# Two layers on one core: the input arrives in column quarters, the first weight slot in halves, and the values' projection takes its low-part products last

## The chip, the cores and the metric

The kernel runs on one core of one Trainium2 chip. The metric is the device time of one execution in microseconds (us). TensorE is the matrix engine, VectorE (DVE in the rows) and ScalarE (ACT) are the elementwise engines, GpSimd (POOL) and SyncE (SP) issue transfers here, and GpSimd does some elementwise work as well.

## The reference, cut to what matters

The input x is 512 tokens by 1024 columns, float32. Two layers follow each other: a mixer (short convolution and dilated attention) with a gated feed-forward part, and then a second hybrid layer (state-space mixer and sparse attention). The change touches the first steps of the first layer only:

```python
h = rms_norm(x, g_mix)                      # per token, times a gain per column
z = h @ w_in                                # 1024 -> 3072 columns
u, gb, gc, q, k, v = jnp.split(z, splits, axis=-1)
q = rms_norm(q.reshape(B, S, N_HEADS, HEAD_DIM), g_q) * HEAD_DIM ** -0.5
k = rms_norm(k.reshape(B, S, N_HEADS, HEAD_DIM), g_k)
```

## The kernel before

**Layout.** Activations stand transposed: `hH` and `hL` hold 8 blocks (index k, `KD` = 8, `KH` = 4) of 128 columns of h on the partitions and all 512 tokens along the free side. `hH` is the block rounded to the type that TensorE multiplies, `hL` what the rounding left. Weights are split the same way: a slot is 128 output columns of a matrix, 128 x 1024 numbers in `raw[par]`; ScalarE's `split_hi` writes `wH[par]` and counts `hi_done`, VectorE's `split_lo` writes `wL[par]` and counts `lo_done`. A projection of a slot is 8 blocks of three products of 128x512: wH by hH, wH by hL, wL by hH. The queries' columns are slot 0, the keys' slot 1, the values' slot 2; slots 3 and on belong to `mix`. The two buffers of each kind are used in turn.

**The norm.** The root of each token's mean square is not applied to x. It is worked out beside the projections (`squares` on VectorE, lines 1241 to 1247 on ScalarE, `newton`), laid on a diagonal (`diag4`), spread over all partitions by one product on TensorE (line 871, in `row_factors`), copied out by ScalarE as `rb` (and squared as `r2b`), and multiplied into the results (`scaled`).

**The transposes.** x arrives by tokens: `x_tok` has 4 tiles (index t, `TB` = 4) of 128 tokens. `x_turn(t, ks)` waits for the transfer of the tile's half and transposes the 128x128 pieces ks into bank `HB[k]`. Block k is complete when the piece of tile 3 is in; then `xn_mm` is counted, ScalarE writes `hH[:, k]` (line 1234, counted in `h1h`), VectorE writes `hL[:, k]` (line 1717, counted in `h1_done`), and TensorE may take its products. `x_copy(k)` takes a copy of the untouched block into `xT`, on ScalarE (counted in `xt_a`) or, for k = 1, on VectorE (`xt_d`). There are only 7 free banks: `HB[7]` is `HB[0]` again, so piece 7 waits until `x_copy(0)` is through.

**Fillers.** Between the first transposes TensorE transposes the identity into a bank that nobody reads (`transposes(PB[6], [ident] * 2)`), and before them it multiplies a tile of ones (line 746).

**Order.** Every engine runs its own list in the order written, and stops at a wait. SP's list: identity, slot 0 (512 KB), columns 0 to 511 of the four tiles (256 KB each), columns 512 to 1023 of the four tiles, slot 1, then a wait for the last tile, slot 2, eleven small rows. GpSimd issues its first transfers after the same wait. TensorE's list: fillers and x_turn of the first half; pieces 4 to 6 of tiles 0 and 1; `project_first` (slot 0: the lines 850 to 852; pieces 4 to 6 of tiles 2 and 3 ahead of block 2, the four pieces 7 ahead of block 4); `project_second` (slot 1: 16 products with wH, lines 860 and 861, then the 8 with wL, line 864); `row_factors` (lines 871 to 877); slot 2 by `project` (lines 655 to 657, three products a block); a small product (line 885) that waits for seven `x_copy` of ScalarE, and `head_sums(0)` (line 770), which take the squares of queries and keys; then `mix(0)` with slot 3.

**ScalarE's list** there: split_hi of slot 0, the eight hH with x_copy(0) behind the fourth, split_hi of slot 1, two rows of squares, two small steps, split_hi of slot 2, x_copy of 3, 2 and 7, then rb, r2b, the squares of queries and keys, split_hi of slot 3, x_copy of 4, 5 and 6. **VectorE's list**: split_lo of slot 0, the eight hL, x_copy(1), two rows of squares, split_lo of slot 1, the steps of the root, diag4, split_lo of slot 2, scaled queries and keys, some small steps, split_lo of slot 3.

Of the kernel before, what the change touches and what calls it, by code (L numbers as in the profile page):

```python
# [16 lines left out]
F32 = mybir.dt.float32  # L17
# [111 lines left out]
def program(nc, io):  # L129
# [7 lines left out]
    with ExitStack() as ctx:  # L137
# [10 lines left out]
        def sem(name):  # L148
# [121 lines left out]
        cst_in, mask_in, glu_full, vec_in, vecp_in, svec_in, s5_in, out_done = (  # L270
            sem(n) for n in ("cst_in", "mask_in", "glu_full", "vec_in", "vecp_in", "svec_in", "s5_in", "out_done"))
# [44 lines left out]
        fin = [sem(f"fin{t}") for t in range(TB)]  # L316
# [46 lines left out]
        def _(sp_):  # L363
# [61 lines left out]
            def at_(i, last):  # L425
# [3 lines left out]
                for e in range(2):  # L429
                    dst = raw[s.par][:].rearrange("p (k e c) -> p k e c", k=KH, e=2)[:, :, e, :]  # L430
                    src = w_glu_2[0].rearrange("(k p) c -> p k c", p=P)[:, :, bass.ds(i * P + e * HALF, P)]
                    sp_.dma_start(dst, src).then_inc(glu_full if e else w_full[s.par], 16)
# [14 lines left out]
            for t in range(TB):  # L447
                sp_.wait_ge(fin[t], 2)
# [176 lines left out]
        def _(pe):  # L625
# [110 lines left out]
            def x_turn(t, ks):  # L736

                pe.wait_ge(x_in[t][ks[0] // KH], 16)
# [98 lines left out]
            def project_first():  # L837

                pe.wait_ge(lo_done, 1)
                pe.wait_ge(vec_cp, 1)  # L840
                for k in range(KD):
                    if k == 2:
                        x_turn(2, range(KH, KD - 1))
                        x_turn(3, range(KH, KD - 1))
                    if k == KH:
                        pe.wait_ge(xt_a, 1)
                        for t in range(TB):
                            x_turn(t, [KD - 1])
                    pe.wait_ge(h1_done, k + 1)
# [5 lines left out]
            def project_second():  # L855

                pe.wait_ge(hi_done, 2)
                pe.wait_ge(xt_d, 1)
                for k in range(KD):
                    mm(PB[1][:], blk(wH[1], k), hH[:, k, :], start=(k == 0), stop=False)  # L860
                    mm(PB[1][:], blk(wH[1], k), hL[:, k, :], start=False, stop=False)
                pe.wait_ge(lo_done, 2)
                for k in range(KD):
                    ins = mm(PB[1][:], blk(wL[1], k), hH[:, k, :], start=False, stop=(k == KD - 1))
# [328 lines left out]
        def _(act):  # L1193
# [30 lines left out]
            def x_copy(k):  # L1224
                act.wait_ge(h1_done, k + 1)
# [24 lines left out]
            for k in (3, 2, 7):  # L1250
                x_copy(k)
# [292 lines left out]
            act.wait_ge(glu_full, 16)  # L1544
# [5 lines left out]
            def att(i, first, last):  # L1550
# [9 lines left out]
                if not last:  # L1560
                    act.wait_ge(glu_full, i * 16 + 32)
# [69 lines left out]
            def token_scale(j, t):  # L1631

                act.wait_ge(r_fin, j + 1)
                A(out_tok[:, t, HALF:D], out_tok[:, t, HALF:D], ACT.Copy, scale=sm[:, 4 + t:5 + t]).then_inc(fin[t], 1)
# [21 lines left out]
        def _(dve):  # L1656
# [833 lines left out]
            def token_scale(t):  # L2490

                TS(out_tok[:, t, 0:HALF], out_tok[:, t, 0:HALF], sm[:, 4 + t:5 + t], None, MU).then_inc(fin[t], 1)
# [32 lines left out]
```

## Time and profile before

| what | value |
|---|---|
| median of 3 runs | 979.25 us (977.92 to 979.74) |
| the profiled execution, its own time | 977.83 us |
| its span, first to last instruction | 976.2 us |
| TensorE busy in it | 963.0 us |
| first product of slot 0 starts | 11.52 us |
| first product of slot 1 / of slot 2 starts | 18.22 / 24.90 us |
| the load for the small product of line 885 starts | 30.61 us |

The profiled execution is 1.6 us longer than its span, which is what lies outside the instructions. Times in a timeline row are the start and the length; of a run of n equal instructions the length runs from the first start to the last end. The matmuls overlap each other, so the distance between two starts, not the length of one, is what a product costs. A bracket at the end of a row says how long the engine stood idle before it and what released it.

### The profile page before, as it was taken

Reading aid. Unit: us, or ns where it says so; the run is one execution under the profiler, and the core shown is the slowest. Engines: PE = TensorE matmul, PEld = TensorE weight load, DVE = VectorE, ACT = ScalarE, POOL = GpSimd, SP = SyncE. Lnnn points to the kernel's source line nnn. Section 1 sums busy time; section 2 is a strip of 40 time slices with the busy share of each in tenths; the row PEclk is TensorE's granted clock in tenths of the full one; section 3 lists DMA queues with packets and bytes.
Section 4 is the critical chain, followed back from the end, with each engine's and each line's share of the span. In section 5 each row is a group of like instructions: output and inputs, shape, how many; then the busy total and the mean of one; then the engine's idle time right before and its main releaser. Section 6 shows DMA issues by size and latency. Waiting matters only on the chain.

```text
span 976.2 us, 13908 instructions
## 1 busy us (share of the span) xinstructions
PE 963.0 (99%) x4623; PEld 776.4 (80%) x4623; DVE 685.5 (70%) x1227; ACT 412.6 (42%) x683; POOL 187.8 (19%) x321
## 2 busy tenths in 40 slices
PE   8999999999999999999999999999999999999996
PEld 7777777687888888888888886888888887677886
DVE  5886795797766666655336568489889876785756
ACT  5564353644323332323221226955652325663234
POOL 3010111120100000187200001745680220100000
PEclk9999999999999999999999999999999999999999
DMA  7346757332653332334322323333233463653222
GB/s 231 112 94 192 208 167 190 74 96 82 182 173 105 95 98 88 104 105 133 137 102 92 102 77 98 97 87 87 60 92 88 120 160 85 146 153 123 86 87 108
DMA packets 143766, 115.13 MB, mean 118 GB/s; under 512 B 5516, under 2 KB 131724, under 8 KB 143724
## 3 DMA queue, kind: packets, MB, share of 16 engines
q1 hardware_dynamic: 135468, 85.88, 29.7%
q0 software_dynamic: 8240, 28.73, 11.0%
q8 instruction: 21, 0.34, 0.1%
q14 instruction: 21, 0.17, 0.1%
q10 hardware_dynamic: 16, 0.00, 0.0%
HBM read 100.44 MB, written 4.20 MB: 107 GB/s over the span
## 4 chain that ended last, share of the span: by engine, by line
PE 95%; DVE 2%; ACT 1%; DMA 1%; issue 0%; SPq 0%; DVEq 0%; ACTq 0%
PE bank L655 19%; PE bank L656 19%; PE bank L657 19%; PE bank L938 4%; PE bank L937 4%; PE bank L939 4%; PE bank L638 2%; PE bank L640 2%; PE bank L639 2%; PE bank L689 2%; PE bank L709 2%; PE bank L1154 1%; PE bank L1152 1%; PE bank L1153 1%; PE bank L824 1%; PE bank L826 1%
## 5 line engine op out<-in xcount | busy, mean ns | idle before, releaser
L655 PE MATMUL bank<-hH,wH 128*128 128x512 f32 x792 | 310.5, 392 | 0.8 <-DVE gt L1980 0.8
L657 PE MATMUL bank<-hH,wL 128*128 128x512 f32 x792 | 308.3, 389 | 0.0
L656 PE MATMUL bank<-hL,wH 128*128 128x512 f32 x792 | 308.2, 389 | 0.0
L1671 DVE TENSOR_TENSOR wL<-raw,wH 128x1024 fp32r<-128x1024 f32 x155 | 195.5, 1262 | 139.5 <-ACT wH L1197 139.2
L1197 ACT ACTIVATE wH<-raw 128x1024 fp32r<-128x1024 f32 x155 | 164.1, 1058 | 289.7 <-PE bank L657 126.2
L655 PEld LDWEIGHTS bank<-hH,wH 128*128 128x128 f32 x792 | 148.7, 188 | 39.1 <-issue 7.9
L657 PEld LDWEIGHTS bank<-hH,wL 128*128 128x128 f32 x792 | 148.7, 188 | 31.0
L656 PEld LDWEIGHTS bank<-hL,wH 128*128 128x128 f32 x792 | 148.7, 188 | 30.1
L937 PE MATMUL bank<-aH,wH 128*128 (+1 forms) x160 | 62.2, 389 | 0.0
L938 PE MATMUL bank<-aL,wH 128*128 (+1 forms) x160 | 62.2, 389 | 0.0
L939 PE MATMUL bank<-aH,wL 128*128 (+1 forms) x160 | 62.2, 389 | 0.0
L1984 DVE TENSOR_TENSOR ut<-bank,r 128x512 f32<-128x512 f32 x22 | 15.2, 691 | 48.9 <-PE bank L657 48.9
L475 POOL DMA_DIRECT2D pTd<-turned x24 | 13.1, 561 | 136.0 <-DVE turned L1820 53.6
L1286 ACT ACTIVATE L<-L,nmx 128x128 f32<-128x128 f32 (+3 forms) x64 | 35.0, 557 | 0.4 <-DVE nmx L1815 0.4
L937 PEld LDWEIGHTS bank<-aH,wH 128*128 128x128 f32 x160 | 30.0, 188 | 6.3
L939 PEld LDWEIGHTS bank<-aH,wL 128*128 128x128 f32 x160 | 30.0, 188 | 6.3
L938 PEld LDWEIGHTS bank<-aL,wH 128*128 128x128 f32 x160 | 30.0, 188 | 6.1
L481 POOL DMA_DIRECT2D mraw<-in_w_mod_dram x24 | 13.3, 554 | 109.7 <-DVE macc L1846 109.7
L548 POOL COPY yaF<-yg 32x128 f32<-32x128 f32 x64 | 33.4, 521 | 2.9
L1197 ACT ACTIVATE aH<-a 128x512 f32 (+1 forms) x22 | 13.9, 632 | 45.2 <-DVE a L1988 45.2
L1153 PE MATMUL bank<-wH,hL 128*128 128x256 f32 (+1 forms) x96 | 30.6, 318 | 0.0
L1154 PE MATMUL bank<-wL,hH 128*128 128x256 f32 (+1 forms) x96 | 30.6, 318 | 0.0
(494 smaller groups left out, 1568.2 us busy)
## 6 DMA issues: line engine op xcount, KB each, us to landing
raw<-in_w_in_dram SPq DMA_DIRECT2D x61, 512.0 KB, 3.6
mraw<-in_w_mod_dram POOLq DMA_DIRECT2D x24, 512.0 KB, 5.1
raw<-in_w_gate_dram SPq DMA_DIRECT2D x22, 512.0 KB, 3.7
raw<-in_w_up_dram SPq DMA_DIRECT2D x22, 512.0 KB, 3.7
raw<-in_w_down_dram SPq DMA_DIRECT2D x22, 512.0 KB, 3.3
raw<-in_w_out_dram SPq DMA_DIRECT2D x16, 512.0 KB, 3.5
pTd<-turned POOLq DMA_DIRECT2D x24, 320.0 KB, 6.9
x_tok<-in_x_dram SPq DMA_DIRECT2D x8, 256.0 KB, 6.2
```

The source lines that it names most:

```text
L548: ins = g.tensor_copy(dst(a, b), src(a, b))
L655: mm(o, a, hH[:, k, :], start=(k == 0), stop=False)
L656: mm(o, a, hL[:, k, :], start=False, stop=False)
L657: ins = mm(o, b, hH[:, k, :], start=False, stop=(k == KD - 1))
L937: mm(PB[d][:], blk(wH[s], d), rh, start=a, stop=False, skip_group_check=True)
L938: mm(PB[d][:], blk(wH[s], d), rl, start=False, stop=False, skip_group_check=True)
L939: ins = mm(PB[d][:], blk(wL[s], d), rh, start=False, stop=False, skip_group_check=True)
L1153: mm(o, hL[:, f, blkc(t)], w, start=False, stop=False, skip_group_check=True)
L1154: ins = mm(o, hH[:, f, blkc(t)], wl, start=False, stop=(f == last), skip_group_check=True)
L1197: return A(o, i_, ACT.Copy, scale=scale)
L1286: ins = A(l, l, ACT.Exp, bias=nmx[:, c:c + 1], scale=-1.0, accum_out=rs[:, c:c + 1])
L1671: TT(wL[s.par][:], raw[s.par][:], wH[s.par][:].bitcast(F32), SU).then_inc(lo_done, 1)
```

## The change

On SP the input comes as columns 0 to 255 of the four tiles, then the first half of slot 0 (blocks k = 0 to 3), columns 256 to 511 of the tiles, the second half of slot 0, and columns 512 to 1023. ScalarE and VectorE split slot 0 by halves, one behind hH and hL of block 0, one behind those of block 3; the counts of `h1h` and `h1_done` move on by one for it, which `h1h_count` and `h1_count` allow for. TensorE turns pieces 0 and 1 of all tiles and 2 and 3 of tiles 0 and 1 ahead of `project_first`, the others inside it: 2 and 3 of tiles 2 and 3 ahead of block 1, 4 to 7 of tile 0 ahead of block 2, of tile 1 ahead of block 3, of tiles 2 and 3 ahead of block 4. ScalarE's x_copy of 3 and 2 moves ahead of hH of block 4, VectorE's x_copy(1) ahead of hL of block 4. Slots 1 and 2 both take their 16 products with wH first and the 8 with wL last, and `row_factors` stands ahead of block 2 of slot 2 and no more between the slots. The counters `glu_full` and `fin` give way to `w_part` and `x_in_fin`, whose later waits are raised by what the new uses count.

```diff
-            load(Slot(N_MIX), cols(w_in, Z_Q))
-            for h in range(2):
+            def query_half(h, done):
+                c = slice(h * KH, h * KH + KH)
+                sp_.dma_start(raw[0][:].rearrange("p (k c) -> p k c", k=KD)[:, c, :], cols(w_in, Z_Q)[:, c, :]).then_inc(done, 16)
+
+            def x_columns(first, n, done):
                 for t in range(TB):
-                    c = slice(h * HALF, h * HALF + HALF)
-                    sp_.dma_start(x_tok[:, t, c], x[0, t * P:(t + 1) * P, c]).then_inc(x_in[t][h], 16)
+                    c = slice(first, first + n)
+                    sp_.dma_start(x_tok[:, t, c], x[0, t * P:(t + 1) * P, c]).then_inc(done(t), 16)
+            x_columns(0, QD, lambda t: x_in[t][0])
+            query_half(0, w_part)
+            x_columns(QD, QD, lambda t: x_in_fin[t])
+            query_half(1, w_full[0])
+            x_columns(HALF, HALF, lambda t: x_in[t][1])
...
             for t in range(TB):
-                x_turn(t, range(KH))
+                x_turn(t, range(KH // 2))
                 transposes(PB[6], [ident] * 2)
-            transposes(PB[6], [ident] * 2)
-            x_turn(0, range(KH, KD - 1))
-            x_turn(1, range(KH, KD - 1))
+            transposes(PB[6], [ident] * 4)
+            for t in range(2):
+                x_turn(t, range(KH // 2, KH))
+                transposes(PB[6], [ident] * 2)
...
             def project_first():
-                pe.wait_ge(lo_done, 1)
                 pe.wait_ge(vec_cp, 1)
                 for k in range(KD):
-                    if k == 2:
-                        x_turn(2, range(KH, KD - 1))
-                        x_turn(3, range(KH, KD - 1))
+                    if k == 1:
+                        x_turn(2, range(KH // 2, KH))
+                        x_turn(3, range(KH // 2, KH))
+                    if k in (2, 3):
+                        pe.wait_ge(xt_a, 1)
+                        x_turn(k - 2, range(KH, KD))
                     if k == KH:
-                        pe.wait_ge(xt_a, 1)
-                        for t in range(TB):
-                            x_turn(t, [KD - 1])
-                    pe.wait_ge(h1_done, k + 1)
+                        x_turn(2, range(KH, KD))
+                        x_turn(3, range(KH, KD))
+                        pe.wait_ge(lo_done, 1)
+                    pe.wait_ge(h1_done, h1_count(max(k, 1)) if k else 2)
...
-            def project_second():
-
-                pe.wait_ge(hi_done, 2)
-                pe.wait_ge(xt_d, 1)
+            def project_low_last(s, bank, between=None):
+
+                pe.wait_ge(hi_done, s.n + 1)
                 for k in range(KD):
...
+                    if k == KH // 2 and between is not None:
+                        between()
...
             project_first()
-            project_second()
-            row_factors()
+            pe.wait_ge(xt_d, 1)
+            project_low_last(Slot(1), PB[1])
             pe.wait_ge(xt_a, 3)
-            project(Slot(2), bank=PB[2])
+            project_low_last(Slot(2), PB[2], row_factors)
...
+            def query_high(h):
+                c = slice(h * HALF, h * HALF + HALF)
+                act.wait_ge((w_part, w_full[0])[h], 16)
+                copy(wH[0][:, c], raw[0][:, c]).then_inc((h1h, hi_done)[h], 1)
...
-            split_hi(Slot(0))
             act.wait_ge(vec_cp, 1)
             for k in range(KD):
                 act.wait_ge(xn_mm, k + 1)
                 A(hH[:, k, :], HB[k][:], ACT.Identity, scale=vec[:, V_GMIX + k:V_GMIX + k + 1]).then_inc(h1h, 1)
+                if k == 0:
+                    query_high(0)
+                if k == 1:
+                    x_copy(0)
                 if k == KH - 1:
-                    x_copy(0)
+                    query_high(1)
+                    x_copy(3)
+                    x_copy(2)
...
-            for k in (3, 2, 7):
-                x_copy(k)
+            x_copy(7)
...
-            split_lo(Slot(0))
+            def query_low(h):
+                c = slice(h * HALF, h * HALF + HALF)
+                dve.wait_ge((h1h, hi_done)[h], 2 - h)
+                TT(wL[0][:, c], raw[0][:, c], wH[0][:, c].bitcast(F32), SU).then_inc((h1_done, lo_done)[h], 1)
...
             for k in range(KD):
-                dve.wait_ge(h1h, k + 1)
+                dve.wait_ge(h1h, h1h_count(k))
                 STT(hL[:, k, :], HB[k][:], vec[:, V_GMIX + k:V_GMIX + k + 1], hH[:, k, :].bitcast(F32), MU, SU
                     ).then_inc(h1_done, 1)
-            x_copy(1)
+                if k == 0:
+                    query_low(0)
+                if k == KH - 1:
+                    query_low(1)
+                    x_copy(1)
```

## Rows read from the trace of the kernel before

**Rows 1.** The page: busy time, share of the span and instructions of TensorE.
```profile
PE 963.0 (99%) x4623; PEld 776.4 (80%) x4623; DVE 685.5 (70%) x1227; ACT 412.6 (42%) x683; POOL 187.8 (19%) x321
```

**Rows 2.** Stages: busy us (count) of each engine, granted clock, DMA share, GB/s.
```profile
2.00:4.00 2.00, 1.73 (x8) 1.73 (x9) 0.22 (x3) 1.32 (x2) 2.00 (x2) 1.00 0.69 183
4.00:6.00 2.00, 2.00 (x10) 1.75 (x10) 0.14 (x1) 0.09 (x1) 0.10 (x1) 1.00 1.05 294
```

**Rows 3.** Stages: the same columns, first products to the last ones of V.
```profile
11.50:30.60 19.10, 19.10 (x88) 15.00 (x86) 16.59 (x28) 15.31 (x27) 5.33 (x10) 1.00 0.60 179
```

**Rows 4.** Timeline of TensorE, us from the start, until the first transposes.
```profile
5.76 0.69 PE L631 MATMUL bank<-cst 128*128 128x128 f32 x2
6.59 0.66 PE L631 MATMUL bank<-cst,x_tok 128*128 128x128 f32 x4
7.08 0.38 PE L631 MATMUL bank<-cst 128*128 128x128 f32 x2
7.30 0.64 PE L631 MATMUL bank<-cst,x_tok 128*128 128x128 f32 x4
...
9.39 0.65 PE L631 MATMUL bank<-cst,x_tok 128*128 128x128 f32 x4 [0.58 <-DMA x_tok<-in_x_dram]
```

**Rows 5.** Timeline of TensorE, from the first product of slot 0 on.
```profile
11.52 0.47 PE L850 MATMUL bank<-hH,wH 128*128 128x512 f32 x1
...
12.98 0.82 PE L631 MATMUL bank<-cst,x_tok 128*128 128x128 f32 x6
13.55 0.48 PE L850 MATMUL bank<-hH,wH 128*128 128x512 f32 x1
...
18.22 0.39 PE L860 MATMUL bank<-hH,wH 128*128 128x512 f32 x1
...
23.67 1.02 PE L871 MATMUL bank<-diag,ones 128*128 128x512 f32 x2
...
24.90 0.50 PE L655 MATMUL bank<-hH,wH 128*128 128x512 f32 x1
```

**Rows 6.** Timeline of the weight loads: the first one behind V.
```profile
30.61 0.30 PEld L885 LDWEIGHTS bank<-sm,identP 128*128 128x128 f32 x2 [0.41 <-ACT xT L1197]
```

**Rows 7.** Timeline of ScalarE: high parts of the input, first copy of it.
```profile
9.82 2.42 ACT L1234 ACTIVATE hH<-bank,vec 128x512 fp32r<-128x512 f32 x4 [2.85 <-PE bank L631]
12.11 0.61 ACT L1197 ACTIVATE xT<-bank 128x512 f32<-128x512 f32 x1
13.62 1.84 ACT L1234 ACTIVATE hH<-bank,vec 128x512 fp32r<-128x512 f32 x3 [0.89 <-PE bank L631]
```

**Rows 8.** Timeline of ScalarE, the row factor out of its bank.
```profile
24.73 0.60 ACT L1197 ACTIVATE rb<-bank 128x512 f32<-128x512 f32 x1 [1.42 <-PE bank L871]
```

**Rows 9.** Timeline of VectorE: low parts of the input, then of weights.
```profile
10.62 2.73 DVE L1717 SCALAR_TENSOR_TENSOR hL<-bank,vec,hH 128x512 fp32r<-128x512 f32 x4 [2.40 <-ACT hH L1234]
14.34 2.79 DVE L1717 SCALAR_TENSOR_TENSOR hL<-bank,vec,hH 128x512 fp32r<-128x512 f32 x4 [0.99 <-ACT hH L1234]
...
20.19 1.22 DVE L1671 TENSOR_TENSOR wL<-raw,wH 128x1024 fp32r<-128x1024 f32 x1
...
25.36 0.69 DVE L1709 TENSOR_TENSOR qraw<-bank,rb 128x512 f32<-128x512 f32 x1 [0.99 <-ACT rb L1197]
...
30.71 1.22 DVE L1671 TENSOR_TENSOR wL<-raw,wH 128x1024 fp32r<-128x1024 f32 x1
```

**Rows 10.** Timeline of the SP queue: first weight slot and the input.
```profile
1.43 0.42 SPq L373 DMA_DIRECT2D raw<-in_w_in_dram  x1
1.90 4.33 SPq L379 DMA_DIRECT2D x_tok<-in_x_dram  x8
```

**Rows 11.** DMA issues, KB each, us from issue to landing: the first weight slot.
```profile
raw<-in_w_in_dram SPq DMA_DIRECT2D x1, 512.0 KB, 4.5
```

**Rows 12.** DMA issues, KB each, us from issue to landing: the first input tile.
```profile
x_tok<-in_x_dram SPq DMA_DIRECT2D x1, 256.0 KB, 4.6
```

**Rows 13.** DMA issues, KB each, us from issue to landing: the last two input tiles.
```profile
x_tok<-in_x_dram SPq DMA_DIRECT2D x2, 256.0 KB, 6.7
```

More of the change, by code:

```diff
@@ L269, in program @@
         x_in = [[sem(f"x_in{t}{h}") for h in range(2)] for t in range(TB)]
-        cst_in, mask_in, glu_full, vec_in, vecp_in, svec_in, s5_in, out_done = (
-            sem(n) for n in ("cst_in", "mask_in", "glu_full", "vec_in", "vecp_in", "svec_in", "s5_in", "out_done"))
+        x_in_fin = [sem(f"x_in_fin{t}") for t in range(TB)]
+        cst_in, mask_in, w_part, vec_in, vecp_in, svec_in, s5_in, out_done = (
+            sem(n) for n in ("cst_in", "mask_in", "w_part", "vec_in", "vecp_in", "svec_in", "s5_in", "out_done"))
         w_full = [sem(f"w_full{s}") for s in range(2)]
@@ L315, in program, with x_part, h1h_count, h1_count @@
             sem(n) for n in ("g_out", "rows_in", "tk_ev", "tk_mm", "x3t", "tsq", "tsum", "f_ln", "f_rs"))
-        fin = [sem(f"fin{t}") for t in range(TB)]
+        def x_part(t, k):
+            return x_in[t][1] if k >= KH else x_in_fin[t] if k >= KH // 2 else x_in[t][0]
+        def h1h_count(k):
+            return 1 if k == 0 else k + 2
+        def h1_count(k):
+            return 1 if k == 0 else k + 2
         def wait(eng, s, v):
@@ L431, in at_ @@
                     src = w_glu_2[0].rearrange("(k p) c -> p k c", p=P)[:, :, bass.ds(i * P + e * HALF, P)]
-                    sp_.dma_start(dst, src).then_inc(glu_full if e else w_full[s.par], 16)
+                    sp_.dma_start(dst, src).then_inc(w_part if e else w_full[s.par], 16)
                 if not last:
@@ L447, in _ @@
             for t in range(TB):
-                sp_.wait_ge(fin[t], 2)
+                sp_.wait_ge(x_in_fin[t], 18)
                 sp_.dma_start(out[0, t * P:(t + 1) * P, :], out_tok[:, t, :]).then_inc(out_done, 16)
@@ L736, in x_turn @@
             def x_turn(t, ks):
-                pe.wait_ge(x_in[t][ks[0] // KH], 16)
+                pe.wait_ge(x_part(t, ks[0]), 16)
                 for k in ks:
@@ L853, in project_first @@
                 ins.then_inc(slot_used, 1)
-            def project_second():
-                pe.wait_ge(hi_done, 2)
-                pe.wait_ge(xt_d, 1)
+            def project_low_last(s, bank, between=None):
+                pe.wait_ge(hi_done, s.n + 1)
                 for k in range(KD):
-                    mm(PB[1][:], blk(wH[1], k), hH[:, k, :], start=(k == 0), stop=False)
-                    mm(PB[1][:], blk(wH[1], k), hL[:, k, :], start=False, stop=False)
-                pe.wait_ge(lo_done, 2)
+                    if k == KH // 2 and between is not None:
+                        between()
+                    mm(bank[:], blk(wH[s.par], k), hH[:, k, :], start=(k == 0), stop=False, skip_group_check=True)
+                    mm(bank[:], blk(wH[s.par], k), hL[:, k, :], start=False, stop=False, skip_group_check=True)
+                pe.wait_ge(lo_done, s.n + 1)
                 for k in range(KD):
-                    ins = mm(PB[1][:], blk(wL[1], k), hH[:, k, :], start=False, stop=(k == KD - 1))
+                    ins = mm(bank[:], blk(wL[s.par], k), hH[:, k, :], start=False, stop=(k == KD - 1), skip_group_check=True)
                 ins.then_inc(slot_used, 1)
@@ L1543, in _ @@
             gate(s, tga[:, KD - 1, :])
-            act.wait_ge(glu_full, 16)
+            act.wait_ge(w_part, 32)
             split_hi(s.next())
@@ L1560, in att @@
                 if not last:
-                    act.wait_ge(glu_full, i * 16 + 32)
+                    act.wait_ge(w_part, i * 16 + 48)
                 split_hi(s.next())
@@ L2490, in token_scale @@
             def token_scale(t):
-                TS(out_tok[:, t, 0:HALF], out_tok[:, t, 0:HALF], sm[:, 4 + t:5 + t], None, MU).then_inc(fin[t], 1)
+                TS(out_tok[:, t, 0:HALF], out_tok[:, t, 0:HALF], sm[:, 4 + t:5 + t], None, MU).then_inc(x_in_fin[t], 1)
             token_last(0)
```

4 lines of the change are left out of this document (2 added, 2 removed).

## The prediction, made before the changed kernel was run

> **What bounds the kernel now.** I read the page first: TensorE is busy 99% of the span [rows 1], so only a change in TensorE's own list, or in the time at which it gets going, can move the end. The stages then show that from the first product of slot 0 to the end of slot 2 TensorE is busy 19.10 of 19.10 us at a granted clock of 1.00 [rows 3]. What lies ahead of 11.52 us is start-up: fillers and transposes [rows 4], and the transfers, which run at 183 and then 294 GB/s [rows 2]. The change wants to shorten this start-up. So I follow TensorE's list, in starts of instructions, from 5.76 to the load at 30.61 us [rows 4 to 6], with the two engines that feed it beside it [rows 7 to 9]. Everything behind 30.61 is taken to shift as a whole.
>
> **Prices from the rows.** Two fillers cost 0.22 us (7.08 to 7.30), four transposes 0.49 (6.59 to 7.08) [rows 4], six transposes queued inside the projection 0.57 (12.98 to 13.55), so 0.095 each; 24 products 5.45 (18.22 to 23.67), so 0.227 each and 0.68 a block; two blocks with an interruption ahead 1.46 (11.52 to 12.98), so 0.78 for the first of them [rows 5]. ScalarE makes hH every 0.60 us (four in 2.42) and takes about 0.60 for a copy of 128x512 [rows 7]; VectorE makes hL every 0.68 (four in 2.73) and takes 0.69 for a 128x512 subtraction or product [rows 9]; half a slot is that size. Behind a queued transpose the chain to TensorE is: six transposes start at 12.98, the piece of block 4 in tile 3 is the fourth, at 13.27; hH at 13.62, hL at 14.34 [rows 5, 7, 9], and hL is usable 0.90 after its start (10.62 to 11.52) [rows 5, 9]: 1.97 us in all. At the start of the kernel it was 9.39 to 11.52, 2.13 [rows 4, 5].
>
> **Do the transfers come in time?** The identity and slot 0, 0.59 MB, had landed at 1.43 + 4.5 = 5.9 us [rows 10, 11]; with the first tile, 0.85 MB, it was 1.90 + 4.6 = 6.5 [rows 10, 12]. In the new order 0.59 MB is the identity and the first quarter of all four tiles, 0.85 MB takes in the first half of slot 0. The quarters take four issues for that instead of one. At 0.5 us an issue (eight in 4.33 [rows 10]) the fourth goes out at about 2.9, and 2.9 plus the 4.5 of rows 11 is 7.4 as an upper bound. TensorE needs tile 0's quarter at 5.98 (5.76 plus two fillers) and tile 3's, behind three lots of two transposes and two fillers (0.25 + 0.22 each), at 7.39. So it is in time, or just. ScalarE needs the first half of slot 0 at 8.4. The last tiles landed at 5.6 + 6.7 = 12.3 [rows 10, 13]; with five more issues (2.3 us) and the same bytes ahead they may come at 12.5 to 14.6, and TensorE asks for them at 15.0 (below). The transfers of the changed order thus bound nothing; slot 1 lands near 14 to 16 and is split at 18.4. Slot 2's transfer now waits for the second half's split (14.2, before 12.3) and has until 22.3; the eleven small rows behind it on SP leave 2 us later and are read near 27. GpSimd's small transfers wait for the same last tile. These I cost at nothing.
>
> By the Trainium skill ("DMA: Bandwidth & Descriptors", Measured under Bandwidth) small transfers are poor ones: batch to 1 MiB, 64 KB reaches 32% of the peak. That speaks against quarters of 128 KB. This trace shows eight transfers of 256 KB in flight together at 294 GB/s and more; the rule is about one at a time, and I weigh it as a rival below.
>
> **First product.** Tile 3's piece at 7.39; hH 0.43 later (9.39 to 9.82), 7.82; hL 0.80 behind (9.82 to 10.62), 8.62, done 9.30 [rows 4, 7, 9]. ScalarE's high half runs 8.42 to 9.02 under that. Then VectorE makes the low half of the slot, 0.65, to 9.95, and TensorE starts 0.22 later (hL started 10.62, plus 0.68, against 11.52): **10.17 us, 1.35 sooner**. TensorE's second lots (tiles 0 and 1) and their fillers end near 9.1 and are hidden.
>
> **Inside project_first.** Here the list of TensorE decides. Before, 10 of the 32 pieces were turned after the first product, each at least two blocks ahead of its use. Now 20 are, some right ahead of the block that the chain behind them releases.
> - Block 0: 10.17 to 10.95. Pieces 2 and 3 of tiles 2 and 3: 0.38; tile 3's piece 2 is the third, at 11.14. Block 1: 11.33 to 12.11. Tile 0, four pieces: to 12.49. Block 2 can't start before 11.14 + 1.97 = 13.11: **a hole of 0.62**.
> - Block 2 to 13.89, tile 1 to 14.27, block 3 to 15.05 (its hL is ready at 13.8). Then eight pieces to 15.81, of which tile 3's piece 4 is the fifth, at 15.43. Block 4 can't start before 17.40: **a hole of 1.59**. I take 17.37 with the roundings.
> - ScalarE has high half, x_copy(3) and x_copy(2) (to 14.8), VectorE low half and x_copy(1) (to 14.9) before that and neither is late. hL of blocks 5 to 7 come every 0.68, TensorE's own pace, so slot 0 ends at 17.37 + 0.78 + 3 x 0.68 = **20.19, before 18.22: 1.97 later**.
> The sum agrees: -1.35, +0.95 for ten more pieces inside, +2.21 for the holes, +0.1 to 0.2 for more interruptions.
>
> **Slots 1 and 2.** Slot 1's 24 products run 20.19 to 25.64. ScalarE's high part is there at 19.4. VectorE, 1.55 later than before (hL 7 at 18.5, then the squares without x_copy(1)), has the low part at 20.19 + 1.22 + 1.55 = 22.96 [rows 9]; it is wanted at 23.8. The low part of slot 2 would come at 25.9, so low-last saves a wait of 0.3 that the old order would have had.
> But row_factors moves behind four products of slot 2 (0.91). It takes 1.23 (23.67 to 24.90) either way. From its product to the load behind slot 2 ScalarE's chain lasted 23.67 to 30.61 = 6.94 us: rb at 24.73, its square, then queries and keys as VectorE delivers them (25.36), the split of slot 3, three copies. Row 6 names the last copy as what released that load, so there is no slack [rows 5, 6, 8, 9]. Now: 25.64 + 0.91 + 6.94 = **33.49**. TensorE is done with slot 2 at 26.55 + 1.23 + 20 x 0.227 + 0.1 = 32.42 and stands **1.07 us**. x_copy of 3, 2 and 7 don't help: they lay ahead of rb. VectorE's list to slot 3's low part (30.71 before) hangs on rb too and shifts alike [rows 9].
>
> **Sum.** 33.49 - 30.61 = +2.88 us. The profiled execution took 977.83 for a span of 976.2; the new one should take 980.7. The median is 979.25, 1.4 above the profiled execution; with the same shift it becomes **982.1 us**. What a measurement can tell from no change is about 0.2%, 1.96 us, so slower is above 981.2.
>
> **Rivals.**
> 1. *The late row factors are hidden*, by a ScalarE list with slack that the profile doesn't show. Then +1.8, 981.05: just no change. Against it: the named releaser and 6.94 us without a pause over 0.3. Chance 0.10.
> 2. *No holes*: the chain from transpose to product is shorter when it is not the first, so that only counts of instructions decide. Then -1.35 + 0.95 + 0.15 + 1.07 = +0.8, 980.1. Against it: the 1.97 has two rows on it at 0.35 and 0.72. Chance 0.12.
> 3. *Faster*: the early start is kept whole, because TensorE's transposes fill waits that it has anyway and ScalarE's chain hides the rest. With -1.35 kept it is 977.9, within 0.2%. It is faster by more only if block 0 starts before 11.52 - 1.96 = 9.56; that would need tile 3's first quarter turned at 6.8, but the list puts three lots ahead of it from 5.98. As a mechanism: the fillers cost less than 0.22 a pair when data is there. Chance 0.08, of a time near 977.
> 4. *The quarters come late*: at half the rate of rows 2, the 0.59 MB need 2.65 us longer, tile 3's quarter lands at 8.6 instead of 5.9, 1.2 behind its need, and all follows: 983.3. Chance 0.06. The skill's rule above gives this case; the rows don't bear it out.
> 5. *The clock falls in the holes*: from 2.4 to 1.2 GHz while TensorE waits 1.59 us, and the 12 products of blocks 4 to 7 take 0.227 longer each: +2.7, 984.8. For it: less work than before up to 17 us. Against it: 1.00 in every row, with 5.9 us of transposes and gaps ahead of 11.52. Chance 0.04. The Trainium skill ("TensorE: Matmul & The Clock Gate", Part 4) says that transposes don't count as busy as matmuls do; by that the clock could have fallen before 11.52 already, and rows 2 and 3 don't show it.
> The forecast has 0.60.
>
> **How the numbers follow.** Own range of the forecast: the holes by a chain of 1.85 to 2.13 (-0.2, +0.3), the first product from 10.0 to 10.9, the wait of 1.07 by 0.3: +2.2 to +4.0, 981.4 to 983.3. The median itself moves by 1 us. The range takes in rivals 1, 2 and 4 and leaves out 3 and 5, with 0.7 us for the measurement at the low end and 1.1 at the high one: 979.4 to 984.4. Slower: 0.56 of the forecast's 0.60, with 0.06 and 0.04 of rivals 4 and 5: 0.66. Same: 0.04, 0.10, 0.12, and a little of rival 3: 0.28. Faster: 0.06.
>
> **What would show it.** First product of slot 0 at 10.0 to 10.4; TensorE idle 0.6 us ahead of block 2 and 1.6 ahead of block 4, released by VectorE's hL; first product of slot 1 at 20.2; load of line 885 at 33.5, idle 1.1 ahead of it, released by an xT copy; the rest of the trace shifted by 2.9. It would be wrong if the first product came under 9.6 or the holes were absent, or if a later stage had slack that took the shift up; no row shows a wait of TensorE for something that doesn't shift along.

## The result, and the profile after

The changed kernel takes 981.49 us in the median of 10 runs (980.56 to 982.77); the kernel before, measured beside it, 979.50 us (977.92 to 982.10, 10 runs). The ratio is 1.0021, with a 95% interval of 1.0013 to 1.0030: 2.0 us slower, 1.3 to 2.9. The forecast was 982.1 in a range of 979.4 to 984.4, slower; 981.49 lies only 0.3 above the 981.2 at which the prediction drew the line between the same and slower. The profiled executions lie further apart than the medians: 981.53 against 977.83 us, spans of 980.0 against 976.2. What the traces say of the extra 1.7 us is told in experiments 5 to 7.

TensorE's timeline after, against [rows 4, 5]. The lines that carry the products of slot 0 are now 873 to 875, those of slots 1 and 2 884 to 888, the factors' product 895, the transposes 651.

```profile
7.55 0.38 PE L651 MATMUL bank<-cst,x_tok 128*128 128x128 f32 x2
...
10.23 0.47 PE L873 MATMUL bank<-hH,wH 128*128 128x512 f32 x1 [0.77 <-DVE wL L1749]
...
11.36 0.48 PE L873 MATMUL bank<-hH,wH 128*128 128x512 f32 x1
...
12.44 0.63 PE L651 MATMUL bank<-cst,x_tok 128*128 128x128 f32 x4
13.06 0.50 PE L873 MATMUL bank<-hH,wH 128*128 128x512 f32 x1
...
14.99 1.03 PE L651 MATMUL bank<-cst,x_tok 128*128 128x128 f32 x8
17.36 0.47 PE L873 MATMUL bank<-hH,wH 128*128 128x512 f32 x1 [1.33 <-DVE hL L1754]
...
20.19 0.39 PE L884 MATMUL bank<-hH,wH 128*128 128x512 f32 x1
...
25.63 0.39 PE L884 MATMUL bank<-hH,wH 128*128 128x512 f32 x1
...
26.55 1.02 PE L895 MATMUL bank<-diag,ones 128*128 128x512 f32 x2
```

Tile 3's first quarter is turned at 7.55 and the first product starts at 10.23, where it was 11.52. Then come the two holes. Block 1 starts at 11.36, its third product at 11.91; at 0.23 us a product TensorE could go on at 12.14. Tile 0's pieces follow at 12.44 only, and block 2 at 13.06. The eight pieces of tiles 2 and 3 start at 14.99, take 0.8, and block 4 starts at 17.36 with 1.33 us of idle time in the bracket, released by VectorE's hL. Slot 1 starts at 20.19 (18.22 before), slot 2 at 25.63, the factors' product at 26.55 behind four products.

The weight loads, against [rows 6]; line 909 is the small product behind slot 2:

```profile
33.48 0.30 PEld L909 LDWEIGHTS bank<-sm,identP 128*128 128x128 f32 x2 [1.32 <-ACT xT L1221]
```

The load that started at 30.61 now starts at 33.48, with 1.32 us ahead of it in place of 0.41, and the same releaser, ScalarE's copy into xT. ScalarE and VectorE, against [rows 7 to 9]:

```profile
7.92 0.69 ACT L1262 ACTIVATE hH<-bank,vec 128x512 fp32r<-128x512 f32 x1 [4.53 <-PE bank L651]
...
11.53 1.27 ACT L1262 ACTIVATE hH<-bank,vec 128x512 fp32r<-128x512 f32 x2 [1.34 <-PE bank L651]
...
15.74 2.42 ACT L1262 ACTIVATE hH<-bank,vec 128x512 fp32r<-128x512 f32 x4 [0.95 <-PE bank L651]
```

```profile
8.74 0.75 DVE L1754 SCALAR_TENSOR_TENSOR hL<-bank,vec,hH 128x512 fp32r<-128x512 f32 x1 [2.71 <-ACT hH L1262]
...
16.46 2.73 DVE L1754 SCALAR_TENSOR_TENSOR hL<-bank,vec,hH 128x512 fp32r<-128x512 f32 x4 [1.60 <-ACT hH L1262]
```

What to see here is how little these two engines do between 10 and 16 us: they wait for TensorE's turns, while TensorE waits for them. The last hH and hL run back to back again, from 15.74 and from 16.46.

### The profile page after: what moved, and what is told of

The parts are those of the page before. It is cut to its first block, busy times and chain, and to the rows that moved or that the text cites. A ratio compares the mean times of both kernels' runs of the same rounds, so it can differ in the third digit from the quotient of the medians.

```text
span 980.0 us, 13929 instructions
## 1 busy us (share of the span) xinstructions
PE 963.7 (98%) x4629; PEld 777.1 (79%) x4629; DVE 685.4 (70%) x1228; ACT 412.8 (42%) x684; POOL 187.2 (19%) x321
## 4 chain that ended last, share of the span: by engine, by line
PE 92%; DVE 4%; ACT 2%; DMA 1%; issue 1%; DVEq 0%; ACTq 0%
PE bank L675 18%; PE bank L677 17%; PE bank L676 17%; PE bank L962 4%; PE bank L961 4%; PE bank L963 4%; PE bank L658 2%; PE bank L660 2%; PE bank L659 2%; PE bank L709 2%; PE bank L729 2%; DMA raw<-in_w_in_dram 1%; PE bank L1178 1%; PE bank L1176 1%; PE bank L1177 1%; PE bank L845 1%
## 5 line engine op out<-in xcount | busy, mean ns | idle before, releaser
L675 PE MATMUL bank<-hH,wH 128*128 128x512 f32 x784 | 307.3, 392 | 1.5 <-DVE gt L2021 0.8
L677 PE MATMUL bank<-hH,wL 128*128 128x512 f32 x784 | 305.2, 389 | 0.0
L676 PE MATMUL bank<-hL,wH 128*128 128x512 f32 x784 | 305.1, 389 | 0.0
L1221 ACT ACTIVATE wH<-raw 128x1024 fp32r<-128x1024 f32 (+1 forms) x156 | 164.3, 1053 | 286.5 <-PE bank L677 127.7
```

The lines of the kernel that those rows point to most:

```text
L675: mm(o, a, hH[:, k, :], start=(k == 0), stop=False)
L676: mm(o, a, hL[:, k, :], start=False, stop=False)
L677: ins = mm(o, b, hH[:, k, :], start=False, stop=(k == KD - 1))
L1221: return A(o, i_, ACT.Copy, scale=scale)
```

## The experiments

There are eleven runs. Eight are parts of the change undone or done alone, or ways on from it; three are the two kernels profiled again. Of the eight, five were timed (1, 2, 4, 10 and 11); the others are one profiled execution each. Timed kernels are given by their ratio to the kernel before on the same chip. As one step is worth about 1 us, 0.1%, and the intervals reach some 0.1% to either side, the timeline decides and the ratio only bears it out.

**1. The factors back between the slots** (`factors_back`):

```diff
             project_low_last(Slot(1), PB[1])
+            row_factors()
             pe.wait_ge(xt_a, 3)
-            project_low_last(Slot(2), PB[2], row_factors)
+            project_low_last(Slot(2), PB[2])
```

> The changed kernel with row_factors back between slots 1 and 2; slot 2 keeps its low-part products last. Theory (ScalarE's chain from the row factors to the load behind slot 2 takes 6.94 us wherever it starts): the product of the factors starts at 25.6 instead of 26.55, the load behind slot 2 at 32.6 instead of 33.48 with about 0.1 us of idle ahead of it instead of 0.90, and the time falls by 0.9 us against the changed kernel, to 1.1 us over the kernel before by medians. Rival (the place of the factors costs nothing; slot 2's end sets it): load at 33.4 to 33.5, no difference.

The load behind slot 2, in the view of the weight loads:

```profile
32.42 0.30 PEld L910 LDWEIGHTS bank<-sm,identP 128*128 128x128 f32 x2 [0.41 <-ACT xT L1222]
```

This execution's first product was at 10.05, so the load comes 22.37 us behind it; in the changed kernel it was 33.48 - 10.23 = 23.25. That is 0.88 sooner, and the idle time is back at the 0.41 that [rows 6] show. The timeline bears the theory out. The time does not: 981.27 us is 1.85 over before on that chip, where 1.1 was expected, a ratio of 1.0025 (1.0016 to 1.0035) beside the 1.0021 of the change. The interval is as wide as the step, and this execution lost 1.0 us at 167 us to a late weight, told of in experiment 7.

**2. One block put into the chain** (`turns_earlier`):

```diff
-                    if k == KH:
+                    if k == KH - 1:
                         x_turn(2, range(KH, KD))
                         x_turn(3, range(KH, KD))
+                    if k == KH:
                         pe.wait_ge(lo_done, 1)
```

> The changed kernel with pieces 4 to 7 of tiles 2 and 3 turned ahead of block 3 instead of block 4, so that block 3 lies inside the chain. Theory (the hole ahead of block 4 is the chain of 1.97 us from tile 3's piece 4): that piece is turned at 14.6 instead of 15.4, block 4 starts at 16.6 instead of 17.36, slot 1 at 19.4 instead of 20.19, 0.75 us off the time. Rival (the last tile's transfer sets block 4; it lands near 14.3): the pieces of tile 3 wait for it, and the gain is under 0.4 us.

TensorE's timeline:

```profile
10.38 0.47 PE L874 MATMUL bank<-hH,wH 128*128 128x512 f32 x1 [0.76 <-DVE wL L1750]
...
14.01 1.47 PE L651 MATMUL bank<-cst,x_tok 128*128 128x128 f32 x12
...
16.81 0.47 PE L874 MATMUL bank<-hH,wH 128*128 128x512 f32 x1 [0.63 <-DVE hL L1755]
```

All twelve pieces go through without a wait from 14.01 on, and block 4 starts 6.43 us behind the first product, where it was 17.36 - 10.23 = 7.13: 0.70 sooner, against 0.75 expected, with 0.63 of the 1.33 left as idle time. The chain sets block 4 and the transfer does not. The ratio is 1.0016 (1.0007 to 1.0025).

**3. The other hole** (`hole1`):

```diff
-            for t in range(2):
+            for t in range(TB):
                 x_turn(t, range(KH // 2, KH))
                 transposes(PB[6], [ident] * 2)
...
-                    if k == 1:
-                        x_turn(2, range(KH // 2, KH))
-                        x_turn(3, range(KH // 2, KH))
```

> The changed kernel with pieces 2 and 3 of tiles 2 and 3 turned ahead of block 0, in TensorE's idle time, instead of ahead of block 1. If the hole ahead of block 2 is the chain alone, block 2 moves from 13.06 to about 12.0. If tile 0's second half, which landed at 6.23 + 6.1 = 12.3, sets it as well, block 2 starts at 12.8 and all behind it 0.25 us sooner, block 4 at 17.1.

```profile
12.58 0.63 PE L651 MATMUL bank<-cst,x_tok 128*128 128x128 f32 x4 [0.68 <-DMA x_tok<-in_x_dram]
12.96 0.48 PE L870 MATMUL bank<-hH,wH 128*128 128x512 f32 x1
...
17.25 0.47 PE L870 MATMUL bank<-hH,wH 128*128 128x512 f32 x1 [1.33 <-DVE hL L1751]
```

With the chain out of the way block 2 moves to 12.96 only (13.06 before the edit), since TensorE now waits by name for tile 0's second half. The first hole has two causes of nearly one size, one behind the other. Taking the chain away is worth 0.1, less than the 0.25 expected. Which of the two ends last in the changed kernel differs between executions: block 2 comes 2.83 us behind the first product there and in experiment 1, and 2.84 in pairs (experiment 8), where TensorE doesn't wait for the transfer and the bracket names hL; in after_again (experiment 7) it waits 0.52 us for the transfer and block 2 comes 2.97 behind.

**4. The values' part alone, on the kernel before** (`values_only`). Slot 2 in the kernel before becomes 16 products with wH, row_factors ahead of block 2, and the 8 with wL last; nothing else changes.

```diff
...
-            row_factors()
             pe.wait_ge(xt_a, 3)
-            project(Slot(2), bank=PB[2])
+            values_low_last()
```

> The kernel before with one part of the change alone: slot 2 takes its low-part products last, with row_factors ahead of its block 2. Theory: the factors' product starts at 24.6 instead of 23.67, the load behind slot 2 at 31.5 instead of 30.61, idle 0.9 to 1.0 ahead of it; the time rises by 0.9 us, 0.09%. Rival (hidden): load at 30.6, no difference.

```profile
32.75 0.30 PEld L897 LDWEIGHTS bank<-sm,identP 128*128 128x128 f32 x2 [1.32 <-ACT xT L1209]
```

The first product was at 12.73 here, so the load comes 20.02 us behind it; before it was 30.61 - 11.52 = 19.09. The part alone costs 0.93 us, with 1.32 idle ahead of the load, as in the changed kernel. Its ratio, 1.0006 (0.9996 to 1.0015), agrees with 0.93 us and doesn't exclude nothing. What I had not expected is the 12.73: the old start-up, untouched by the edit, was 1.2 us later than in [rows 5].

**5 and 6. The kernel before, twice more** (`before_again`, `before_third`, no edit).

> The kernel before once more, for its start-up alone. In values_only, which has the same start-up, tile 3's first half was turned at 10.60 and not at 9.39, and all behind it 1.1 us later. Theory: the old order's first product hangs on a landing that varies by 1 us or more from one execution to the next, and the profiled execution of before was an early one; then the first product is seen anywhere from 11.5 to 12.8. Rival: the delay came from the edit; then it is 11.5 to 11.6 here.

> The kernel before a third time, for its start-up. If the first product varies with the landing of tile 3's first half, it is in 11.5 to 12.8 and follows that tile's turn by 2.13 us.

TensorE's timeline of the one and of the other:

```profile
10.16 0.66 PE L631 MATMUL bank<-cst,x_tok 128*128 128x128 f32 x4 [0.65 <-DMA x_tok<-in_x_dram]
...
12.29 0.47 PE L850 MATMUL bank<-hH,wH 128*128 128x512 f32 x1
```

```profile
9.30 0.66 PE L631 MATMUL bank<-cst,x_tok 128*128 128x128 f32 x4 [1.28 <-DMA x_tok<-in_x_dram]
...
10.76 0.66 PE L631 MATMUL bank<-cst,x_tok 128*128 128x128 f32 x4 [0.58 <-DMA x_tok<-in_x_dram]
...
12.88 0.47 PE L850 MATMUL bank<-hH,wH 128*128 128x512 f32 x1
```

The first product is at 12.29 and 12.88, and follows tile 3's turn (10.16, 10.76) by 2.13 and 2.12 us, as it did at 9.39 [rows 4]. In before_third the brackets name the transfers of x that TensorE waits for. So the old order's start is set by a landing that varies, and in four executions it was 11.52, 12.29, 12.73 and 12.88. The profiled execution that I worked from was the earliest. The load behind slot 2 in before_third:

```profile
31.97 0.30 PEld L885 LDWEIGHTS bank<-sm,identP 128*128 128x128 f32 x2 [0.41 <-ACT xT L1197]
```

In before_again it was at 31.41. The mean of the three executions of the kernel before is 31.33, 0.7 us later than [rows 6]. Behind that load the three are alike: span less load is 945.6, 945.6 and 945.9 us.

**7. The changed kernel once more** (`after_again`, no edit).

> The changed kernel once more. Its first product does not hang on a landing, but on TensorE's list and the two engines behind it: 10.0 to 10.9 as in its four relatives (10.05, 10.23, 10.38, 10.87), block 4 follows it by 7.1, the load behind slot 2 at 33.3 to 34.1. The wait of 0.8 us at 167 us for a weight that came late may be absent, as it is in turns_earlier.

First product at 9.84, 0.16 earlier than I had bounded it; block 4 at 17.10, 7.26 behind it where 7.1 was expected, as tile 0's transfer came 0.14 us too late for block 2; load at 33.24, just under the 33.3 to 34.1. The mean of 33.48 and 33.24 is 33.36, and 33.36 - 31.33 = 2.0 us, the distance of the medians.

The profiled changed execution also lost 0.7 us later on. The waits between 150 and 172 us:

```profile
ACT wH L1221 <- DMA raw<-in_w_in_dram: 8.5, 1, 8.5
...
PE bank L675 <- DVE wL L1704: 0.7, 1, 0.7
```

ScalarE waited 8.5 us for a weight, and VectorE's low part was 0.7 late for TensorE. In after_again that transfer was waited for 5.6 us (in the first execution of the kernel before 5.8) and TensorE did not wait at all. It shows in factors_back (1.0) and in values_only (0.9), and in no other trace at this place. It comes and goes between executions of the changed kernel. Whether the change makes it more frequent is open: of the three traces of the kernel before none has it.

So the distance of the two profiled executions, 3.7 us, is 2.87 at the load, 0.7 of the late weight and 0.1 of rest. That the means of three and of two traces give just the 2.0 of the medians is agreement and no proof. The timed executions of the kernel before reach over 3 us (977.9 to 981.0 on the chip of experiments 1 and 2), the landings in its traces over 1.4, so something else varies too, and how often a median execution meets a late weight was not measured.

**8. Fewer transfers for the same bytes** (`pairs`). The changed kernel with the quarters of two tiles in one transfer.

```diff
...
+            def x_pairs(first, n, done):
+                for t in (0, 2):
+                    c = slice(first, first + n)
+                    sp_.dma_start(x_tok[:, t:t + 2, c], x[0, t * P:(t + 2) * P, c].rearrange("(t p) c -> p t c", p=P)).then_inc(done(t), 16)
-            x_columns(0, QD, lambda t: x_in[t][0])
+            x_pairs(0, QD, lambda t: x_in[t][0])
             query_half(0, w_part)
-            x_columns(QD, QD, lambda t: x_in_fin[t])
+            x_pairs(QD, QD, lambda t: x_in_fin[t])
...
```

> The changed kernel with the quarters of tiles 0 and 1 in one transfer, and of 2 and 3 in one: 10 issues ahead of slot 1 and not 14, the rows in DRAM that a packet reads still 1 KB. If the 14 issues at 0.48 us hold the transfers back (they moved at 230, 268 and 223 GB/s from 4 to 10 us, where the old order had 294, 360 and 295), the rates return to about 300 and the last tile lands near 12.7 and not at 14.3. If the 1 KB rows do it, rates and landing stay. Block 4 hangs on the chain in either case and stays at 17.2 to 17.4.

Stages of the changed kernel, then of pairs; the last two columns are the DMA share and GB/s:

```profile
4.00:6.00 2.00, 2.00 (x10) 1.75 (x10) 0.14 (x1) 0.00 (x0) 0.10 (x1) 1.00 0.76 230
6.00:8.00 2.00, 2.00 (x19) 2.00 (x19) 0.03 (x1) 0.08 (x1) 0.00 (x0) 1.00 0.90 268
8.00:10.00 2.00, 1.46 (x14) 1.22 (x12) 1.26 (x2) 2.00 (x4) 0.00 (x0) 1.00 0.88 223
```

```profile
4.00:6.00 2.00, 2.00 (x10) 1.75 (x10) 0.14 (x1) 0.00 (x0) 0.10 (x1) 1.00 0.88 255
6.00:8.00 2.00, 2.00 (x13) 2.00 (x13) 0.03 (x1) 0.00 (x0) 0.00 (x0) 1.00 0.91 282
8.00:10.00 2.00, 2.00 (x20) 1.87 (x18) 0.62 (x1) 1.43 (x3) 0.00 (x0) 1.00 1.04 350
```

230, 268 and 223 GB/s become 255, 282 and 350, the first two less than the 300 expected. The last tile's transfer is issued near 6.25 and takes 6.4 us, so it lands near 12.6; in the changed kernel it was issued near 7.65 and took 6.6, landing near 14.3. So it was mostly the number of issues (10 for 14) that held the transfers back and not the 1 KB rows. The kernel gains nothing by it: block 4 came at 18.00, 7.13 behind a first product at 10.87, exactly the changed kernel's distance. The chain is the bound, and a transfer that is 1.7 us sooner lands in the hole.

**9 and 10. Two versions to fill the holes** (`best_two`, `best_all`): pairs, the fillers behind the first turns, all second quarters turned ahead of block 0, the second half of slot 0 issued behind the last tile, the later turns moved ahead of block 2 or 3, factors back. The main lines of best_all:

```diff
...
+            x_columns(HALF, HALF, lambda t: x_in[t][1])
             query_half(1, w_full[0])
-            x_columns(HALF, HALF, lambda t: x_in[t][1])
...
-                    if k in (2, 3):
+                    if k == KH // 2:
                         pe.wait_ge(xt_a, 1)
-                        x_turn(k - 2, range(KH, KD))
+                        for t in range(TB):
+                            x_turn(t, range(KH, KD))
                     if k == KH:
-                        x_turn(2, range(KH, KD))
-                        x_turn(3, range(KH, KD))
...
```

> pairs, and: fillers between the first turns put behind them, all second quarters turned ahead of block 0, tiles 0 and 1 of the second half ahead of block 2, tiles 2 and 3 ahead of block 3, row_factors back between the slots, and the second half of slot 0 issued behind the last tile. Chain theory: first product 9.5, the tiles land by 12, block 4 at 14.9, slot 1 at 17.7, load behind slot 2 at 30.1. Rival (landings of the second half bind instead): slot 1 at 18.2 to 18.8.

> best_two, with the second half of all four tiles turned ahead of block 2, so that two blocks lie in the chain. Chain theory: block 4 at 13.9 to 14.2, slot 1 at 17.0, load behind slot 2 at 29.5, which is 1.1 us sooner than in the profiled execution of before and up to 2 sooner than its usual one: 977.5 to 978.5. Rival (landings bind, last tile at 12.5 or later): block 4 at 14.9 or later, slot 1 at 17.7 to 18.3, no difference from before that can be told.

Both miss. best_all is slower than the kernel before: 982.65 us, 1.0030 of it (1.0019 to 1.0041); its ten executions reach from 979.5 to 984.08, and the profiled one is the slowest. Its TensorE and VectorE:

```profile
12.07 1.91 PE L655 MATMUL bank<-cst,x_tok 128*128 128x128 f32 x16
...
16.39 0.47 PE L873 MATMUL bank<-hH,wH 128*128 128x512 f32 x1 [1.02 <-DVE hL L1755]
...
26.88 1.13 PE L895 MATMUL bank<-diag,ones 128*128 128x512 f32 x2 [2.03 <-DVE diag L1776]
```

```profile
25.03 0.29 DVE L1768 COPY row<-ldt 16x64 f32<-16x64 f32 x2 [3.13 <-DMA ldt<-in_log_dt_dram]
...
26.13 0.69 DVE L1776 TENSOR_TENSOR diag<-cst,sm 128x512 f32<-128x512 f32 x1 [0.15 <-DVE sm L1719]
```

Block 4 is no sooner than 16.39, as ScalarE sits at the second half of slot 0, which I had put last (idle 1.45 us, at 13.27), and hH of block 4 stands behind it. And a new wait takes the gain back: VectorE waits 3.13 us for `ldt`, one of the small rows behind slot 2 on SP. diag4 comes at 26.13, and TensorE idles 2.03 us ahead of the factors' product. In best_two the same waits are 2.7 and 1.65 us.

SP is hardly later for it: ldt went out at 18.87, against 18.58 in the changed kernel. It took 6.1 us, against 3.0. The queues of GpSimd and SP in best_all:

```profile
16.98 1.09 POOL L505 DMA_DIRECT2D mraw<-in_w_mod_dram  x2
```

```profile
18.87 0.53 SPq L411 DMA_DIRECT2D ldt<-in_log_dt_dram  x1
```

GpSimd sends its transfers once the last tile is there, and with pairs that is 2 us sooner. Its two transfers of 512 KB into mraw now go out 1.9 us ahead of ldt; in the changed kernel they went out at 18.92, behind it. The traces agree on this: in the three with mraw 1.9 to 2.2 us ahead (pairs, best_two, best_all) ldt takes 5.7 to 6.1 us, in nine others mraw goes out with ldt or up to 0.4 us behind it, and ldt takes 2.7 to 3.7; in four_quarters, where ldt goes out 3.6 us ahead of mraw, it takes 1.6. It was not tested by moving mraw alone. In pairs itself the late row costs nothing, as the factors' product stands four products later there.

The wait cost best_all more than its 2.03 us. TensorE behind it, and the stage's granted clock (third figure from the right):

```profile
28.77 0.63 PE L885 MATMUL bank<-hL,wH 128*128 128x512 f32 x1
29.20 0.63 PE L884 MATMUL bank<-hH,wH 128*128 128x512 f32 x1
```

```profile
29.00:30.00 1.00, 1.00 (x3) 0.78 (x3) 1.00 (x3) 0.73 (x2) 0.00 (x0) 0.50 0.47 128
```

The granted clock is 0.50, the lower of TensorE's two levels, and two products are 0.43 us apart where they were 0.23; the fast pace is back at 31.74. From the factors' product to the load it is 35.15 - 26.88 = 8.27 us, 1.33 more than the usual 6.94. In best_two, with 1.65 us of waiting, the clock stayed at 1.00.

**11. All four quarters** (`four_quarters`). The input entirely in quarters of two tiles (10 issues), a quarter turned at least a block ahead of its use, the three rows that VectorE needs ahead of slot 2, the copies where the kernel before has them:

```diff
...
+            x_pairs(0)
             query_half(0, w_part)
...
+            x_pairs(1)
             query_half(1, w_full[0])
...
+            x_pairs(2)
+            x_pairs(3)
...
-            for t in range(TB):
-                x_turn(t, range(KH // 2))
-                transposes(PB[6], [ident] * 2)
...
+            for q in range(2):
+                for t in range(TB):
+                    x_turn(t, range(2 * q, 2 * q + 2))
+                if q == 0:
+                    for _ in range(2):
+                        transposes(PB[6], [ident] * 4)
...
                     if k in (2, 3):
                         pe.wait_ge(xt_a, 1)
-                        x_turn(k - 2, range(KH, KD))
+                        for t in range(TB):
+                            x_turn(t, range(2 * k, 2 * k + 2))
...
```

> All of the input as quarters, two tiles to a transfer (10 issues ahead of slot 1); first two quarters turned ahead of block 0 with the fillers behind the first, third quarter ahead of block 2, fourth ahead of block 3, so that each block's pieces are turned at least one block ahead and what the chain of 1.97 us needs is covered; row_factors between the slots; ScalarE's and VectorE's copies where the kernel before has them; the three small rows that VectorE needs issued ahead of slot 2. Chain theory: first product 9.6 to 10.3, hole under 0.5 us in all, slot 1 at 17.3 to 17.8, load behind slot 2 at 29.8 to 30.3. That is 1 to 2 us sooner than the kernel before in its usual start (31.4), and 977.5 to 978.5 on a chip where before has 979. Rival (something else is late, as the small rows were in best_all): idle time of TensorE ahead of the factors' product or of slot 2's low parts.

```profile
9.36 0.48 PE L874 MATMUL bank<-hH,wH 128*128 128x512 f32 x1
...
10.83 1.03 PE L657 MATMUL bank<-cst,x_tok 128*128 128x128 f32 x8
11.62 0.48 PE L874 MATMUL bank<-hH,wH 128*128 128x512 f32 x1
...
12.39 1.04 PE L657 MATMUL bank<-cst,x_tok 128*128 128x128 f32 x8
13.19 0.48 PE L874 MATMUL bank<-hH,wH 128*128 128x512 f32 x1
...
16.68 0.39 PE L885 MATMUL bank<-hH,wH 128*128 128x512 f32 x1
...
22.13 1.02 PE L896 MATMUL bank<-diag,ones 128*128 128x512 f32 x2
```

```profile
29.07 0.30 PEld L911 LDWEIGHTS bank<-sm,identP 128*128 128x128 f32 x2 [0.41 <-ACT xT L1223]
```

First product at 9.36, no hole behind it, slot 1 at 16.68, factors at 22.13, the load at 29.07: 1.5 us sooner than [rows 6] and 2.3 sooner than the mean of before. All three came sooner than expected (9.6, 17.3 and 29.8 at the earliest). 977.54 us (12 runs) against 978.93 on that chip, a ratio of 0.9985 (0.9976 to 0.9994): 1.4 us faster than the kernel before, as forecast. The profiled execution, 976.39, is the fastest of the twelve, which fall into a group near 976.5 and one near 978.7 with few between; what parts them no trace shows, so the 2.3 us at the load are its best case. Several edits came together here, and their shares were not parted.

## Why the prediction was right, point by point

- **First product.** 10.17 forecast, 10.23 and 9.84 measured. The fillers set TensorE's pace up to it and two engines the rest, and the transfers of the first quarter weren't waited for.
- **Hole ahead of block 2.** Forecast 0.62 by the chain alone, block 2 at 13.11; it came at 13.06. Half of the idle time lay ahead of tile 0's turn (12.14 to 12.44), for which the prediction had no wait: it gave landings for the last tiles and none for tile 0's second half, issued at 6.2 and 6.1 us under way, 12.3. In this execution that lies inside the chain, and the mechanism holds (2.83 us behind the first product, as in the executions where the transfer isn't waited for). That it held was luck by a margin of 0.1 us: in after_again the transfer ended last and cost 0.14, and in experiment 3 it takes the place of the chain at once.
- **Hole ahead of block 4.** Forecast start 17.37, measured 17.36 and 17.10; experiment 2 moves it by 0.70 for a predicted 0.75, and experiment 8 keeps it at 7.13 behind the first product with the transfers 1.7 us sooner. This step is shown.
- **Slots 1 and 2.** 20.19 and 25.64 forecast, 20.19 and 25.63 measured.
- **Late factors.** 6.94 us from the factors' product to the load forecast; 33.48 - 26.55 = 6.93, and 6.94 or 6.95 in all other traces but best_two (7.05) and best_all. Undone it gives 0.88 back, alone on the kernel before it costs 0.93. Shown twice on the timeline; the timed medians are too coarse for it. TensorE's idle time ahead of the load was 0.9 us, where 1.07 was forecast.
- **The sum.** +2.88 forecast at the load, +2.87 measured against the same execution of before. That all behind the load shifts as a whole holds too: span less load is 945.6 to 945.9 us in nine of the thirteen traces, and 945.7 to 945.8 in three more once their late weight is taken off. The thirteenth is best_all, at 947.3.
- **From there to the median** one step was off: that the median shifts by what the profiled execution shifts by. It moved by 2.0. The execution of [rows 4 to 6] had an early start; the mean of three is 0.7 later, which would account for most of the difference, though so few traces don't prove it (experiment 7). I wrote that the transfers bound nothing in the new order and did not turn that around: the old order hangs on a landing, and a landing varies. The profile had shown it, by the 0.58 us bracket at 9.39 that names the transfer [rows 4].
- **Small rows behind slot 2 at nothing.** True for the change, but experiments 9 and 10 show how thin that cover is: once GpSimd's large transfers went out ahead of them, they cost TensorE 1.65 and 2.03 us, and the clock in the second case.
- **Rivals.** Hidden factors (1) and no holes (2) are refuted by experiments 1, 2 and 4. The early start was not kept whole (3). The quarters landed in time (4). The clock did not fall in the changed kernel's holes (5): blocks 4 to 7 run at 0.23 us a product behind 1.33 us of idle time. But the mechanism is real in this kernel, as best_all shows behind its 2.03 us, so a longer hole might have brought it.

## What to carry to other kernels

An early first product is worth nothing if the pieces behind it are turned right ahead of their use: with a chain of 2 us through two engines, each piece needs 2 us of other work between its turn and its product (here three blocks, or as in four_quarters two blocks and the eight pieces of another quarter), and that has to be written into the list of the engine that stops in order. When a shared step (here the row factors) feeds the longest chain of another engine, moving it back costs its full delay, though its own engine has other work to do meanwhile. A transfer that lands sooner also lets loose what another engine sends behind it, and that can make a small transfer late. And before a shift is added to a median, see whether the start of the profiled execution hangs on a landing: two or three more profiled executions of the kernel before show how far it moves.

## What the runs showed of the hardware that I had not expected

- Transfers of 128 KB issued by one queue came out every 0.48 us and the engines were busy 0.76 to 0.90 of the time at 223 to 268 GB/s; with the quarters in transfers of 256 KB, with the same 1 KB rows, it was 255 and 282 from 4 to 8 us, and 350 from 8 to 10, where the halves with 2 KB rows are under way.
- The same transfers, in the same start-up, landed up to 1.4 us apart between executions (tile 3's first half turned at 9.39, 10.16, 10.60 and 10.76).
- A small transfer of 0.1 KB took 5.7 to 6.1 us from issue to landing where another queue had sent 1 MB 1.9 to 2.2 us ahead of it, and 2.7 to 3.7 us where that went out about with it or behind it; a slot of 512 KB on its own queue stood ahead of it in both.
- TensorE's granted clock fell to 0.50 behind an idle time of 2.03 us (best_all), and not behind 1.65 us (best_two) or 1.33 us (the changed kernel).
- Early transposes ran at half their pace in some executions. In pairs two of them took 0.43 us until about 7.5 us and 0.22 afterwards:

```profile
7.09 0.62 PE L655 MATMUL bank<-cst,x_tok 128*128 128x128 f32 x2
7.52 0.41 PE L655 MATMUL bank<-cst 128*128 128x128 f32 x2
...
7.98 0.38 PE L655 MATMUL bank<-cst 128*128 128x128 f32 x2
8.20 0.38 PE L655 MATMUL bank<-cst,x_tok 128*128 128x128 f32 x2
```

  In before_again four took 0.90 (6.61 to 7.51), where [rows 4] have 0.49. The granted clock is given as 1.00 in all of them, though the factor of two is that of TensorE's two levels, 1.2 and 2.4 GHz, and though best_all's products at 0.50 show the same factor. What slowed them I did not test. In the new order it moves the first product, 9.84 to 10.87 in the variants that share it.
